# Scores, turned probabilities and values one weight tile later in the chunks of the hybrid layers

## The reference

```python
proj = h @ w_in                                   # 256 x 1024 times 1024 x some 10,000
(a_b, a_c, a_x, a_z, c_q, c_kv, k_pe, b_z, dq, dk, dv, c_z, gate_pre) = split(proj)
y_a = a_b * conv(a_c * a_x) * silu(a_z)           # causal convolution of three taps
o_b = causal_block_attention(q, k, v)             # 8 heads; q, k, v from c_q, c_kv, k_pe
y_b = o_b * silu(b_z)
o_c = sum over 3 dilations of alpha * dilated_group_attention(dq, dk, dv)   # 8 heads
y_c = o_c * silu(c_z)
g_a, g_b, g_c = split(sigmoid(gate_pre + b_gate))
x = x + (g_a * (y_a @ w_out_a) + g_b * (y_b @ w_out_b) + g_c * (y_c @ w_out_c)) @ w_o
```

## Time and profile before

| | us |
|---|---|
| median of 3 runs | 1363.39 (1362.85 to 1363.47) |
| the profiled execution's own time | 1365.69 |
| its span | 1363.9 |
| TensorE busy | 1339.1 (98%) |
| VectorE busy | 891.7 (65%) |
| ScalarE busy | 705.5 (52%) |
| mean granted TensorE clock | 0.999 |

### The profile page before, as it was taken

The page is one execution under the profiler, slowest core; times in us unless marked ns, Lnnn a source line. Parts: engine busy times, 40 slices in busy tenths (PEclk is TensorE's granted clock), DMA queues, the critical chain, the costliest instruction groups (busy, mean ns, idle before and its releaser), DMA issues.

```text
span 1363.9 us, 17823 instructions
## 1 busy us (share of the span) xinstructions
PE 1339.1 (98%) x7128; PEld 1138.0 (83%) x7128; DVE 891.7 (65%) x1058; ACT 705.5 (52%) x1003; POOL 86.4 (6%) x77
## 2 busy tenths in 40 slices
PE   7999999999999999999999999999999999999998
PEld 5788878988788788888888899888788888998886
DVE  5756556676878755546676557766666865676674
ACT  5544445567646544436766444444367664344451
POOL 0000000000001000001261000000002510000000
PEclk9999999999999999999999999999999999999999
DMA  7866637542466766644656444445466564434552
GB/s 250 277 210 201 207 104 242 156 124 89 144 216 209 256 188 187 193 134 144 219 161 214 135 125 130 150 154 170 155 199 204 169 205 134 124 124 132 160 187 78
DMA packets 64386, 233.88 MB, mean 171 GB/s; under 512 B 7472, under 2 KB 7600, under 8 KB 64176
## 3 DMA queue, kind: packets, MB, share of 16 engines
q1 hardware_dynamic: 61632, 223.90, 52.0%
q10 hardware_dynamic: 2672, 8.84, 1.8%
HBM read 231.66 MB, written 1.05 MB: 171 GB/s over the span
## 4 chain that ended last, share of the span: by engine, by line
PE 85%; DVE 7%; DMA 3%; ACT 2%; issue 1%; POOL 1%; SPq 0%; ACTq 0%; DVEq 0%; POOLq 0%
PE psum L1790 74%; PE psum L1845 5%; PE psum L2000 3%; DMA raw<-weights 3%; PE psum L1983 3%; DVE w_lo L1100 2%; DVE y_lo L1100 1%; DVE tail_lo L1100 1%; ACT y_hi L563 1%; DVE x_lo L1146 1%; DMA res<-x 0%; DVE norm L1138 0%; ACT w_hi L563 0%; PE psum L2084 0%; POOL rstd L508 0%
## 5 line engine op out<-in xcount | busy, mean ns | idle before, releaser
L1100 DVE TENSOR_TENSOR w_lo<-raw,w_hi 128x1024 fp32r<-128x1024 f32 x226 | 274.3, 1223 | 160.9 <-ACT w_hi L563 158.1
L563 ACT ACTIVATE w_hi<-raw 128x1024 fp32r<-128x1024 f32 x226 | 237.1, 1055 | 146.9 <-PE psum L1790 131.0
L1790 PE MATMUL psum<-w_hi,x_hi 128*128 128x512 f32 (+1 forms) x584 | 232.8, 399 | 4.7 <-DVE x_lo L1146 2.4
L1790 PE MATMUL psum<-w_hi,x_lo 128*128 128x512 f32 (+1 forms) x584 | 227.5, 389 | 0.0
L1790 PE MATMUL psum<-w_lo,x_hi 128*128 128x512 f32 (+1 forms) x584 | 227.4, 389 | 0.0
L1100 DVE TENSOR_TENSOR y_lo<-raw,y_hi 128x1024 fp32r<-128x1024 f32 x144 | 175.3, 1222 | 78.7 <-ACT y_hi L563 77.6
L563 ACT ACTIVATE y_hi<-raw 128x1024 fp32r<-128x1024 f32 x144 | 151.5, 1056 | 83.7 <-PE psum L1790 65.1
L1790 PE MATMUL psum<-y_hi,x_hi 128*128 128x512 f32 (+1 forms) x408 | 162.3, 398 | 1.1 <-DVE y_lo L1100 1.1
L1790 PE MATMUL psum<-y_hi,x_lo 128*128 128x512 f32 (+1 forms) x408 | 159.1, 390 | 0.0
L1790 PE MATMUL psum<-y_lo,x_hi 128*128 128x512 f32 (+1 forms) x408 | 158.9, 389 | 0.0
L1790 PEld LDWEIGHTS psum<-w_hi,x_hi 128*128 128x128 f32 x584 | 110.0, 188 | 29.4 <-issue 3.6
(11 more groups left out here) (187 smaller groups left out, 2324.1 us busy)
## 6 DMA issues: line engine op xcount, KB each, us to landing
raw<-weights SPq DMA_DIRECT2D x422, 512.0 KB, 4.0
arena<-gains ACTq DMA_DIRECT2D x7, 512.0 KB, 4.8
arena<-gate_bias ACTq DMA_DIRECT2D x2, 1536.0 KB, 7.8
res<-x SPq DMA_DIRECT2D x2, 512.0 KB, 5.5
arena<-lru_w ACTq DMA_DIRECT2D x1, 1024.0 KB, 4.9
cst<-consts ACTq DMA_DIRECT2D x1, 736.0 KB, 4.9
arena<-gains SPq DMA_DIRECT2D x1, 512.0 KB, 5.1
out<-res SPq DMA_DIRECT2D x1, 512.0 KB, 2.6
```

The lines of the kernel that those rows point to most:

```text
L563: act.activation(slot(t)[0], raw[:, t % RAW, :], ACT.Copy).then_inc(hi_ready, 1)
L1100: dve.tensor_tensor(lo, raw[:, t % RAW, :], hi.bitcast(F32), ALU.subtract).then_inc(lo_ready, 1)
L1790: ins = pe.matmul(out_, a, b, start=start and n == 0, stop=stop and n == 2, skip_group_check=skip)
```

## The change

On all three engines the steps of a unit move one tile down the list, and on VectorE and ScalarE behind the eviction.

```diff
 ScalarE
 for c in range(1, LAYER_CHUNKS + 2):
-    if 1 <= u <= UNITS_LAYER:
-        probs_copy(At(UB + u, l, UNITS_LAYER))
     ... refill(t), eviction ...
+    if 1 <= u <= UNITS_LAYER:
+        probs_copy(At(UB + u, l, UNITS_LAYER))
     refill(t + 1)
...
+    refill(t + 2)
     if 0 <= u < UNITS_LAYER:
         exps(At(UB + u + 1, l, UNITS_LAYER), rows2[u])
-    refill(t + 2)
 VectorE
-    if 1 <= u <= UNITS_LAYER:
-        probs_copy(At(UB + u, l, UNITS_LAYER), 8)
     if c > 1:
         refill(t)
-    if 0 <= u < UNITS_LAYER:
-        ... mask or distance, maximum ...
     ... eviction; for c == 15: conv2((2,)), product, release ...
+    if 1 <= u <= UNITS_LAYER:
+        probs_copy(At(UB + u, l, UNITS_LAYER), 8)
     refill(t + 1)
+    if 0 <= u < UNITS_LAYER:
+        ... mask or distance, maximum ...
...
-    if c == 20:
-        last_values()
     refill(t + 3)
+    if c == 20:
+        last_values()
 TensorE, after tile q of chunk c
-    if q == 0 and 0 <= u < UNITS_LAYER:
+    if q == 0 and 1 <= u <= UNITS_LAYER:
+        if c == 15:
+            pe.wait_ge(heads_lo, At(6, l, 4))
+        turn_probs(At(UB + u, l, UNITS_LAYER), 8)
+    if q == 1 and 0 <= u < UNITS_LAYER:
         ... probs_read(...)
         scores(u, unit_items(u))
-    if q == 1 and 1 <= u <= UNITS_LAYER:
+    if q == 2 and 1 <= u <= UNITS_LAYER:
         unit_values(u - 1)
-    if c == 14 and q == 2:
+    if c == 14 and q == 3:
         pe.wait_ge(max_ready, At(UB + u + 1, l, UNITS_LAYER))
         turn_heads(At(3, l, 2))
-if c == 14:
-    pe.wait_ge(heads_lo, At(6, l, 4))
-if 0 <= u < UNITS_LAYER:
-    turn_probs(At(UB + u + 1, l, UNITS_LAYER), 8)
```

More of the change, by code:

```diff
@@ L1655, in _ @@
                         dil_sum(c - 2)
+                    if 1 <= u <= UNITS_LAYER:
+                        probs_copy(At(UB + u, l, UNITS_LAYER), 8)
                     refill(t + 1)
+                    if 0 <= u < UNITS_LAYER:
+                        un = At(UB + u + 1, l, UNITS_LAYER)
+                        if u < len(UNITS_MLA):
+                            qt, heads = UNITS_MLA[u]
+                            mask_scores(un, qt, len(heads), mask_causal)
+                            negated_max(len(heads), P * (qt + 1)).then_inc(max_ready, 1)
+                        else:
+                            qt, heads = DIL_UNITS[u - len(UNITS_MLA)]
+                            dve.wait_ge(scores_ready, un)
+                            for n, h in enumerate(heads):
+                                for g, lo, hi, at in ((0, 0, 256, 256 * qt), (1, 256, 384, 512), (2, 384, 512, 640)):
+                                    step.mark(dve.scalar_tensor_tensor(
+                                        probs[:, 512 * n + lo:512 * n + hi], dil_dist[:, at:at + hi - lo],
+                                        -slope(g, h), psum[:, 4 + n, lo:hi], ALU.mult, ALU.add))
+                            step.sync()
+                            negated_max(len(heads), 512).then_inc(max_ready, 1)
                     if c == 1:
```

## The result

| | us |
|---|---|
| the changed kernel, median of 4 runs | 1375.07 (1372.35 to 1376.58) |
| the kernel before, 4 runs | 1363.43 (1362.85 to 1364.12) |
| ratio | 1.0083, 95% interval 1.0065 to 1.0101 |
| profiled execution of the changed kernel | 1376.58, span 1374.8, mean granted clock 0.994 |

The four runs with their mean granted clocks are 1376.58 (0.994), 1376.05 (0.995), 1374.10 (0.996) and 1372.35 (0.998): the lower the clock, the longer the run.

What follows compares the result with a forecast made beforehand. TensorE was taken as the bound, busy 1339.1 of 1363.9 us. The median before, 1363.39, plus 6.5 of waits and 2.8 of clock falls gave 1372.7 us, own range 1371.0 to 1374.2, 8 in 10 within 1368.8 to 1375.0.

Steps and rivals of the forecast that it cites:

- No wait to remove in chunks 9 to 20: TensorE in chunks 9 to 20: busy 176.00 of 176.00 and 175.00 of 175.00 us, so nothing to gain there.
- Costs of the moves outside chunk 15 at nothing: Moved steps in the other chunks: distances between steps cover them, so they were costed at nothing.
- The margin of about 1 us foreseen for chunks 17 to 19: Chunks 17 to 19: latest copy together 5.3 us, scores after some 6.4, leaving about 1 us.
- The wait in chunk 15: Chunk 15, each layer: TensorE waits 3.25 us for VectorE's copy before the scores, 6.5 us in two layers.
- T: End of tile 3, just before the turned heads and chunk 15's tile 0; TensorE reaches the scores at T + 7.55.
- The clock: Behind chunk 15's wait the granted clock falls, costing 1.4 us in each layer, 2.8 in all.
- the forecast's own range: Whole kernel: 1371.0 to 1374.2 us, from 2.8 to 3.8 us for each wait and 1.0 to 1.62 for each fall.
- the upper bound of 1375.0: Whole kernel: upper end of the range that should hold 8 in 10, 1368.8 to 1375.0 us.
- the sum: Whole kernel: 6.5 us of waits plus 2.8 of clock, 9.3 us, giving a median of 1372.7.
- The rival by the Trainium skill's reading of the gate: Chunk 15: clock keeps its level, only the waits count, 1363.39 + 6.5 = 1369.9 us; chance 0.15.

Runs made afterwards that it cites:

- e6: The kernel before with TensorE's list of the changed kernel, ScalarE's and VectorE's lists left as before: 1364.42 us, 0.9993 of before.
- e1: The changed kernel with VectorE's copy of the turned probabilities put first in its list in chunk 15: 1364.06 us, 0.9997 of before.
- e3: The kernel before with only VectorE's chunk 15 changed, the copy put behind refill(t), conv2((2,)) and the product: 1378.02 us, 1.0093 of before.
- e5: The changed kernel with VectorE's copy in chunk 15 after refill(t), before conv2((2,)) and the product: 1365.12 us, 1.0007 of before.
- e2: The changed kernel with VectorE's copy in chunk 15 after refill(t) and conv2((2,)), before the product: 1370.48 us, 1.0040 of before.
- e7: The changed kernel with TensorE's list of the kernel before, so only ScalarE's and VectorE's lists are changed: 1397.51 us, 1.0240 of before.
- e4: The changed kernel with 14 useless products added on TensorE in chunk 15, ahead of its wait for the copies: 1371.20 us, 1.0044 of before.
- e9: The kernel before with VectorE's add_product(2, 0) at each layer's end moved ahead of refill(t + 1): 1360.99 us, 0.9974 of before.

## Why the prediction was right, and where a size was off

- *No wait to remove in chunks 9 to 20.* Right: e6 and e1 gain nothing that can be measured.
- *Costs of the moves outside chunk 15 at nothing.* Right: no wait there in the changed kernel, and e1 is at 0.9997. The margin of about 1 us foreseen for chunks 17 to 19 is there: in chunk 17 ScalarE's copy ended at 870.29 + 0.58 = 870.87 and the scores began at 871.91. In e1 it was used up in chunk 16, where TensorE waited 0.47 us.
- *The wait in chunk 15.* Right in place, releaser and order. With T = 829.44 the copy was foreseen at T + 10.07 and began at 839.50, T + 10.06; it ended, as foreseen, 0.69 later. The hand-over to TensorE was 0.14 (the chain's "issue") instead of 0.05, and TensorE came to the scores 0.1 sooner than worked out: 3.43 instead of 3.25. e3 shows it without the rest of the change, e5 and e2 show it step by step.
- *The clock.* This is the term that was mis-sized. The mechanism was right and its size too small: I took 1.4 us for each of the two waits, 2.8 in all; in the profiled execution they cost 1.57 and 2.50, because the second fall lasted about twice as long. What I left out is that the clock can fall at the wait of the second layer's end as well, 1.6 us more in this execution. Two waits 0.18 longer and 1.3 more for the clock give 1372.7 + 0.4 + 1.3 = 1374.4, before the fall at the end. The median was 1375.07: 2.4 above the 1372.7, 0.9 above the forecast's own range and 0.07 above the upper bound of 1375.0. Of the medians' difference of 11.6 us the waits take 6.9 and leave 4.8 where the sum had 2.8. That 1.4 us was a choice between 0 and 1.62, made from two waits of which one brought the clock down; that both new waits would, was not worked out.
- *The rival by the Trainium skill's reading of the gate* ("TensorE: Matmul & The Clock Gate", section "What's actually happening") had the clock up, for 1369.9 us. It fell at both waits of 3.43 us. The falls behind 2.07 us in e2 and behind 1.91 here speak against the reading as I had taken it for this kernel.

What stays open: which waits of about 2 us bring the clock down. 1.91 us did in one execution and not in another at the same place. Counted over the hybrid layers in the traces of all twelve kernels, the clock fell at all 6 waits of 3.43 us or more, at 3 of the 6 between 1.98 and 2.07, at 10 of the 20 of 1.91 or 1.92, and at none of 1.69 or less.

## What to carry to other kernels

When a consumer's step and its producer's step are moved by the same distance, look for the one chunk in which the producer's list holds more than usual: here one copy in each layer behind 4.2 us of other work, two of 22 such copies, made the whole loss. Add up the durations in front of a step on its in-order engine and compare them with the arrival of the engine that waits; in this case that sum was right to 0.2 us for the changed kernel and e3, and in e7 for six of the eight chunks that waited (the other two were 0.24 and 0.31 off). In this kernel, whose TensorE is busy all the time, a new wait of 3.4 us or more cost its length and some 1.6 to 2.5 us of slow clock; one of about 2 us cost 1.6 more in about every second case.

## What the runs showed of the hardware

- TensorE's granted clock fell to its lower level at waits of 1.91 to 2.07 us in 13 of 26 cases, at those of 3.43 to 4.07 us in 6 of 6, not at 0.4 or 1.69 us, and not when the time of a 3.43 us wait was filled with products (e4).
- A fall cost 1.57 to 1.64 us, and 2.50 where it lasted about twice as long. It can begin during the wait (second layer of the changed kernel) or after it (first layer).
- These falls make much of the spread of this kernel's runs: with the waits at the layers' ends cut to 0.8 us (e9) the spread was 1.7 us over 11 runs, against 4.4 over 21 runs of before beside it and 3.6 over the 11 of e1, where these waits are 1.9 us.
